# Computing the Mamba step sizes inside the keys-and-values chunk of a fused two-layer backbone, and reordering the input stage around it

## The chip, the cores and the metric

One core of one Trainium2 chip runs the whole program. The metric is device time of one execution in microseconds. TensorE (PE) does the matrix products, ScalarE (ACT) and VectorE (DVE) read PSUM and write SBUF, GpSimd (POOL) adds a few blocks, SyncE (SP) issues the loads.

## The reference, cut to what matters

Two layers run over 256 latent and 256 context tokens with 1024 features, all in fp32. Each layer starts with one input projection, whose columns go to three mixers:

```python
proj = h @ p['w_in']                    # columns: k, v, xb, dt, C, q, z, hyena
dt = softplus(dt_raw + dt_bias)         # dt_raw: 16 columns, two directions x 8 heads
a_dt = dt * a;  a_cs = cumsum(a_dt)     # decays of the Mamba scan
y = y * silu(z);  y = rmsnorm(y) * g    # gate at the end of the Mamba mixer
```

The three mixers' outputs are normalized, joined, projected and added to the stream; a SwiGLU follows. In layer 1 (the second) the context tokens are needed only for keys, values, the xb columns and dt.

## The kernel before, in words

Every weight is used as a pair: `w_hi` is the raw piece rounded to fp32r by ACT (`round_w`, L1481), and `w_lo` is the rest, which DVE makes (`split_w`, L1854). A product is three matmuls (hi x hi, hi x lo, lo x hi). Weights come in pieces of 512 KB into a ring of four slots (`RING = 4`). SP loads a piece once PE has counted `w_used` for the piece four places back; ACT rounds it, DVE splits it, PE waits for `w_lo_done`.

The input stage of each layer has 30 pieces, two for each of the 15 chunks in `W_IN`: three xb chunks and C (kind `xbc`), then z (two chunks), kv (one), q (two), hyena (six). Products land in two pairs of PSUM banks, (0, 1) and (2, 3). A chunk opens its pair with `pair_open`, which waits until the reader of the chunk before the last has counted `pair_free`. For `xbc` and `hy` chunks ACT starts the short convolution (L1548) and DVE finishes it (L2035, L2039) and frees the pair. A z chunk is read by ACT with Silu (L1557), kv by DVE copies (L2052, L2053).

The first two chunks are made together by `h_pair` (L834, L835, L841), as h becomes ready block by block. Behind it `step_sizes` (L952, L953) makes the 16 step-size columns for all tokens: a 128x32 weight (hi and lo side by side, made by POOL from a load of its own, `load_wdt`) against h_hi and h_lo, 16 matmuls of 512 columns. DVE copies the 32 rows (L2015), PE turns them to tokens with `dsel` (L999), and DVE and ACT make dt, its logarithm and dt·a (L2084 to L2092, L1575 to L1578).

The order of the small work is written out by hand: `at_piece(s)` and `in_piece(s)` on PE, and a loop over s = 2 to 31 on ACT and on DVE, where step s reads the chunk that ended with piece s-1, rounds or splits piece s+2, and then does what the constants assign to it: `S_DT` = 5 the step sizes, `S_CUMS` = 6 cumulative sums (L1004 to L1010, L2121 to L2131), `S_XS0`, `S_XS1`, `S_B` = 7, 8, 9 transposes (L1024), `S_G` = 11 the products of B and C (L1032), `S_HEAD` = 12 the first of eight decay matrices (one for each piece: L963, L965 on PE, L1612 on ACT, L2146, L2147 on DVE, L983 on PE), `S_STATE` = 13 the first of twelve state steps (L1073, L1080, L2154 to L2167), `S_GATE` = 25 the gate (L2240), `S_GATE + 1` the root mean square on ACT (L1462 to L1464), `S_FEAT` = 29 the transposes of the result (L862). In layer 0 five spectra of the Hyena filter are made at pieces 10 to 12 (`filter_spectrum`, L918 and L922, one bank, each copied by DVE at L2116 before the next may start); in DVE's step they come after the `S_DT` work. In layer 0 the projection runs over 512 tokens in every chunk, in layer 1 z, q and hyena run over 256.

Each engine takes its instructions strictly in order. ACT's tables have to be switched between Silu and the set with exponential and logarithm (`ACT_TABLE_LOAD`).

Of the kernel before, what the change touches and what calls it, by code (L numbers as in the profile page):

```python
# [17 lines left out]
P = 128  # L18
D = 1024
# [23 lines left out]
        + [("z", OFF_Z + CW * i, i) for i in range(2)] + [("kv", OFF_K, 0)]  # L43
# [7 lines left out]
STAGES = [("in", 30, 15), ("out", 12, 4), ("gu0", 24, 12), ("down0", 12, 4), ("gu1", 20, 10), ("down1", 12, 4)]  # L51
RING = 4

# [14 lines left out]
def piece_cols(i):  # L68


    for l in range(DEPTH):
        g = PLAN[l, "down1"][0]
        if g <= i < g + 12:
            return CW * (4, 3, 3)[(i - g) % 3]
    return 4 * CW
# [3 lines left out]
S_DT, S_CUMS, S_XS0, S_XS1, S_B, S_G, S_HEAD, S_STATE, S_GATE, S_FEAT = 5, 6, 7, 8, 9, 11, 12, 13, 25, 29  # L79
# [6 lines left out]
SPEC_BANKS = (1, 6, 7, 4, 5)  # L86
# [161 lines left out]
def backbone(nc, x, c, ctx_in, c_ctx, w_mod, b_mod, norm1_g, w_in, ssd_conv_w, ssd_conv_b, ssd_a_log,  # L248
# [3 lines left out]
    with ExitStack() as stack:  # L252
# [12 lines left out]
        w_raw, w_lo = at("w_raw", 48, [RING, 4 * CW]), at("w_lo", 48, [RING, 4 * CW], F32R)  # L265
        w_hi = at("w_hi", 64, [RING, 4 * CW], F32R)
        m_raw = at("m_raw", 80, [2, 4 * CW])
        m_big = [at("m_even", 80, [8 * CW]), at("m_odd", 144, [8 * CW])]


        xbc = at("xbc", 88, [8, T])
        ysum, xw = at("ysum", 88, [4, 512]), at("xw", 96, [2, 512])
        hyv, x0, x1t = at("hyv", 104, [4, T]), at("x0", 112, [4, T]), at("x1t", 120, [2, T])
        zs = at("zs", 124, [4, 512])
        qk, v_nat = at("qk", 132, [4, QKW]), at("v_nat", 142, [4, 2 * HD])
        spec = at("spec", 144, [5, 512])
        csT, csr = at("csT", 154, [T]), at("csr", 154, [T], F32R)
        gT, bnat = at("gT", 156, [2, 4, P]), at("bnat", 160, [4, GN])
        xsn = at("xsn", 164, [4, 512])
        em = at("em", 172, [4, T])  # L280
        st = at("st", 180, [2, 512])


        f_hi, f_lo = at("f_hi", 88, [12, T], F32R), at("f_lo", 112, [12, T], F32R)
        att_lo, hy_lo = at("att_lo", 156, [4, T], F32R), at("hy_lo", 164, [4, T], F32R)
        gate, hidden = at("gate", 136, [2, T]), at("hidden", 140, [2, T])
        sqr, rstd, lnt = at("sqr", 172, [2, T]), at("rstd", 176, [T]), at("lnt", 178, [T])
        hf = at("hf", 180, [2, T])

        c_sq = at("c_sq", 184, [4, P])  # L290
        maskb, identb = at("maskb", 186, [2, P], BF16), at("identb", 186.5, [P], BF16)
        c_fwd = at("c_fwd", 187, [5 * P + 3])
        c_inv = at("c_inv", 193, [2 * NFREQ, P])
        c_rope = at("c_rope", 197, [2, 2, HD])
        gcoss = [at(f"gcos{l}", kb, [2, 2, HD]) for l, kb in enumerate((156, 201.5))]
        gsins = [at(f"gsin{l}", kb, [2, 2, HD]) for l, kb in enumerate((157, 202.5))]
# [4 lines left out]
        wdts = [at(f"wdt{l}", kb, [8, 16]) for l, kb in enumerate((154, 176))]  # L301
        wdt_hl = at("wdt_hl", 201.5, [8, 32], F32R)
# [12 lines left out]
        dsel = at("dsel", 207.6875, [16])  # L315
        hsqs, hbuf = at("hsqs", 112, [2, QKW]), at("hbuf", 112, [2, QKW])
        ropt = at("ropt", 117, [QKW])
        qkT = at("qkT", 132, [4, 5, P])


        t_filt, t_sum, t_diff = at("t_filt", 104, [2, D]), at("t_sum", 112, [2, 512]), at("t_diff", 116, [2, 512])
        t_mod = at("t_mod", 148, [2, CW])
        t_hyb = at("t_hyb", 152, [512])
        t_half, t_hyb1 = at("t_half", 180, [D]), at("t_hyb1", 178, [512])
        t_sum1, t_diff1 = at("t_sum1", 164, [2, 512]), at("t_diff1", 168, [2, 512])

        t_folds = [at(f"t_fold{l}", kb, [4, 512]) for l, kb in enumerate((104, 156))]
        t_w3, t_decay = at("t_w3", 156, [D]), at("t_decay", 160, [2, 512])
        t_arg, t_k, t_h = ([at(f"{name}{l}", kb + off, shape) for l, kb in enumerate((144, 172))]
                           for name, off, shape in (("t_arg", 0, [L]), ("t_k", 1, [L]), ("t_h", 2, [2, L])))  # L330
        t_w1, t_w2, t_feats = at("t_w1", 168, [HD]), at("t_w2", 168.25, [HD]), at("t_feats", 168.5, [L])
        t_mask = at("t_mask", 169.5, [2, P])
        m_acc, m_pick = at("m_acc", 152, [2, MOD_COLS]), at("m_pick", 205, [2, 32])
        m_first = [at(f"m_first{m}", kb, [2, MOD_COLS]) for m, kb in enumerate((80, 112, 120, 128, 136, 88, 96, 104))]
# [4 lines left out]
        vn, yspecs = at("vn", 16, [4, 512]), [at("yspec0", 24, [NFREQ, 512]), at("yspec1", 172, [NFREQ, 512])]  # L339
# [2237 lines left out]
```

## Time and profile before

| | us |
|---|---|
| median of three runs | 1227.86 (1227.34 to 1228.2) |
| the profiled execution: its own time | 1227.09 |
| its span, first to last instruction | 1225.0 |
| PE busy | 1186.8 (97%) |
| DVE busy | 828.6 (68%) |
| ACT busy | 523.9 (43%) |
| POOL busy | 12.5 (1%) |

Times in rows count from the start of the span. In a timeline row the columns are start, duration of the merged group, engine, line, operation, output<-input, shape and count; square brackets hold the idle time of that engine before the row and what released it. A matmul's duration overlaps the next one, so the cost of a group is the distance of the starts. The input stage of layer 0 lies at about 29 to 262 us, that of layer 1 at 796 to 939 us.

### The profile page before, as it was taken

What the parts mean: (1) busy time and instruction counts of PE and PEld (TensorE: products, weight loads), DVE (VectorE), ACT (ScalarE), POOL (GpSimd) and SP (SyncE); (2) the same over time, 40 slices, a digit from 0 to 9 for tenths busy, and PEclk for the clock granted to TensorE, in tenths of its full rate; (3) what the DMA queues carried; (4) which work ended last, traced back from release to release, by engine and by line L of the source; (5) the groups of instructions that cost most, each with busy time, mean ns of one, the idle gap of its engine ahead of it and who ended that gap; (6) DMA issues with size and microseconds to landing.
All of it is one profiled execution on the core that took longest, in us unless ns stands there. A gap on an engine that the chain in (4) does not pass through costs nothing. (4 is left out here: it accounts for less than half of the span.)

```text
span 1225.0 us, 16695 instructions
## 1 busy us (share of the span) xinstructions
PE 1186.8 (97%) x6746; PEld 954.8 (78%) x6746; DVE 828.6 (68%) x1298; ACT 523.9 (43%) x907; POOL 12.5 (1%) x16
## 2 busy tenths in 40 slices
PE   5999999999999999999999999999989998999998
PEld 3667777777677788888887778678888688889888
DVE  5755457869766748677556665575699876776674
ACT  4453544552544532231122232366575555443454
POOL 0000000000000000000000000000000000000000
PEclk9999999999999999999999999999999999999999
DMA  9834243421012255556656454324334133665553
GB/s 337 265 121 137 87 138 123 154 69 52 19 35 70 69 172 187 184 179 206 196 187 198 145 190 155 95 69 123 102 108 134 53 86 100 194 189 184 183 180 125
DMA packets 132388, 171.36 MB, mean 140 GB/s; under 512 B 9268, under 2 KB 112342, under 8 KB 132312
## 3 DMA queue, kind: packets, MB, share of 16 engines
q1 hardware_dynamic: 131828, 170.12, 43.2%
q8 instruction: 53, 0.87, 0.3%
q10 hardware_dynamic: 484, 0.18, 0.1%
q14 instruction: 23, 0.19, 0.0%
HBM read 169.24 MB, written 1.05 MB: 139 GB/s over the span
## 5 line engine op out<-in xcount | busy, mean ns | idle before, releaser
L1854 DVE TENSOR_TENSOR w_lo<-w_raw,w_hi 128x1024 fp32r<-128x1024 f32 (+1 forms) x220 | 264.3, 1206 | 161.9 <-ACT w_hi L1481 159.9
L1481 ACT ACTIVATE w_hi<-w_raw 128x1024 fp32r<-128x1024 f32 (+1 forms) x220 | 228.8, 1043 | 328.2 <-DMA w_raw<-in_w_gu_dram 142.5
L730 PE MATMUL ps<-h_hi,w_hi 128*128 128x512 f32 (+1 forms) x576 | 218.7, 380 | 0.9 <-DVE w_lo L1854 0.6
L732 PE MATMUL ps<-h_hi,w_lo 128*128 128x512 f32 (+1 forms) x576 | 212.7, 369 | 0.0
L731 PE MATMUL ps<-h_lo,w_hi 128*128 128x512 f32 (+1 forms) x576 | 212.4, 369 | 0.0
L730 PE MATMUL ps<-f_hi,w_hi 128*128 128x512 f32 (+1 forms) x472 | 168.0, 356 | 2.7 <-DVE xT L2273 2.5
L732 PE MATMUL ps<-f_hi,w_lo 128*128 128x512 f32 (+1 forms) x472 | 162.8, 345 | 0.0
L730 PEld LDWEIGHTS ps<-h_hi,w_hi 128*128 128x128 f32 x576 | 108.5, 188 | 26.9 <-issue 8.8
L732 PEld LDWEIGHTS ps<-h_hi,w_lo 128*128 128x128 f32 x576 | 108.5, 188 | 18.8
L731 PEld LDWEIGHTS ps<-h_lo,w_hi 128*128 128x128 f32 x576 | 108.6, 189 | 17.4
L741 PE MATMUL ps<-h_hi,w_hi 128*128 128x512 f32 x320 | 113.2, 399 | 0.4 <-ACT gate L1786 0.4
L730 PEld LDWEIGHTS ps<-f_hi,w_hi 128*128 128x128 f32 x472 | 89.6, 190 | 19.3 <-issue 4.7
L732 PEld LDWEIGHTS ps<-f_hi,w_lo 128*128 128x128 f32 x472 | 89.5, 190 | 11.0
L731 PE MATMUL ps<-f_lo,w_hi 128*128 128x512 f32 (+1 forms) x240 | 90.1, 375 | 0.0
L742 PE MATMUL ps<-h_hi,w_lo 128*128 128x256 f32 x320 | 89.9, 281 | 0.0
L741 PEld LDWEIGHTS ps<-h_hi,w_hi 128*128 128x128 f32 x320 | 60.1, 188 | 15.5 <-DVE w_lo L1854 0.6
L742 PEld LDWEIGHTS ps<-h_hi,w_lo 128*128 128x128 f32 x320 | 60.5, 189 | 0.0
L731 PEld LDWEIGHTS ps<-f_lo,w_hi 128*128 128x128 f32 x240 | 45.2, 188 | 8.2 <-issue 0.5
L2491 DVE SCALAR_TENSOR_TENSOR m_acc<-m_odd,cact,m_acc 128x1024 f32<-128x1024 f32 x40 | 50.2, 1281 | 0.5
L1670 ACT ACTIVATE prob<-ps,sm 128x512 f32<-128x512 f32 (+1 forms) x48 | 29.1, 612 | 40.4 <-DVE sm L2315 37.9
L2454 DVE TENSOR_TENSOR hidden<-gate,ps 128x1024 f32<-128x1024 f32 (+1 forms) x12 | 14.1, 1176 | 41.5 <-PE ps L732 38.2
L1132 PE MATMUL ps<-w_hi,h_hi 128*128 128x512 f32 x96 | 40.4, 421 | 0.5 <-DVE xbc L2039 0.5
(349 smaller groups left out, 1904.6 us busy)
## 6 DMA issues: line engine op xcount, KB each, us to landing
w_raw<-in_w_gu_dram SPq DMA_DIRECT2D x88, 512.0 KB, 3.6
w_raw<-in_w_in_dram SPq DMA_DIRECT2D x60, 512.0 KB, 3.8
w_raw<-in_w_down_dram SPq DMA_DIRECT2D x32, 512.0 KB, 3.4
m_even<-in_w_mod_dram SPq DMA_DIRECT2D x14, 1024.0 KB, 6.0
m_odd<-in_w_mod_dram SPq DMA_DIRECT2D x14, 1024.0 KB, 5.9
m_raw<-in_w_mod_dram SPq DMA_DIRECT2D x24, 512.0 KB, 5.3
m_first<-in_w_mod_dram SPq DMA_DIRECT2D x16, 512.0 KB, 10.4
w_raw<-in_w_out_dram SPq DMA_DIRECT2D x16, 512.0 KB, 3.4
```

Source lines behind the costliest of these rows:

```text
L730: mm(o, w_hi[:, i % RING, w], hi[:, 0:n], start=first and k == 0, stop=False)
L731: mm(o, w_hi[:, i % RING, w], lo[:, 0:n], start=False, stop=False)
L732: last = mm(o, w_lo[:, i % RING, w], hi[:, 0:n], start=False, stop=final and k == nk - 1)
L741: mm(o, w_hi[:, i % RING, w], both(k), start=first and k == 0, stop=False)
L742: last = mm(o[:, 0:L], w_lo[:, i % RING, w], both(k)[:, 0:L], start=False, stop=final and k == nk - 1)
L1132: mm(o, h_hi[:, b, tok], w_hi[:, (i + half) % RING, w], start=(b == 0), stop=False)
L1481: A(w_hi[:, i % RING, w], w_raw[:, i % RING, w], ACT.Copy).then_inc(w_hi_done, 1)
L1670: p.sig(A(prob[:, i % 2, j, 0:keys], ps[:, 4 + j, 0:keys], ACT.Exp, bias=sm[:, 0, c:c + 1], accum_out=sm[:, 1, c:c + 1]), "probs_ready")
L1854: TT(w_lo[:, i % RING, w], w_raw[:, i % RING, w], w_hi[:, i % RING, w].bitcast(F32), ALU.subtract).then_inc(w_lo_done, 1)
L2454: TT(hidden[:, :, 0:n], gate[:, :, 0:n], ps[:, 2 * ((q + 1) % 2):2 * ((q + 1) % 2) + 2, 0:n], ALU.mult).then_inc(pair_free[(q + 1) % 2], 1)
L2491: ins = STT(out=acc, in0=src, scalar=by, in1=acc, op0=ALU.mult, op1=ALU.add)
```

## The change

Step sizes stop being a product of their own. The kv chunk becomes `KVW` = 272 columns wide (256 of keys and values, 16 of dt), all ring slots grow to `SLOT` = 1088 columns, and each kv piece is loaded by two DMAs (256 and 16 columns). One token tile with 272 columns fills a bank, so kv takes two pairs instead of one, and the input stage has 16 pairs. kv moves ahead of z (pieces 8 and 9; z at 10 to 13). `load_wdt`, POOL's two operations, `step_sizes`, the copy, `dsel` and the turning matmuls go; DVE adds the bias while it reads kv. `h_pair` ends chunk 0 ahead of chunk 1 in its last three blocks of the second half (it is also used in the SwiGLU stages), and ACT and DVE handle pieces 4 and 5 only after chunk 0's convolution. z is copied from PSUM without Silu and gets it in SBUF at step 22. The hand-written order shifts.

```diff
-        + [("z", OFF_Z + CW * i, i) for i in range(2)] + [("kv", OFF_K, 0)]
+        + [("kv", OFF_K, 0)] + [("z", OFF_Z + CW * i, i) for i in range(2)]
-S_DT, S_CUMS, S_XS0, S_XS1, S_B, S_G, S_HEAD, S_STATE, S_GATE, S_FEAT = 5, 6, 7, 8, 9, 11, 12, 13, 25, 29
+S_DT, S_CUMS, S_XS0, S_XS1, S_B, S_G, S_HEAD, S_STATE, S_ZS, S_GATE, S_FEAT = 10, 11, 7, 8, 9, 12, 13, 14, 22, 26, 29
...
+                    both = (4, 1)[half]
+                    for k in range(both):
...
+                    for k in range(both, 4):
+                        p.after("h_hi_ready")
+                        of_hi(k, 0)
+                        p.after("h_ready")
+                        of_lo(k, 0)
+                    for k in range(both, 4):
+                        of_hi(k, 1)
+                        of_lo(k, 1)
...
                     if s == S_CUMS:
                         p.after("adt_ready")
+                        p.after("xsn_ready", l + 1)
...
                     if s == S_G:
                         p.after("conv_ready")
-                        p.after("xsn_ready", l + 1)
+                        p.after("csr_ready")
+                        p.after("decays_ready")
...
-                step_sizes()
...
+                            if u == count:
+                                pair_open(q + 1)
...
+                            if u == count - 1:
+                                p.sig(last, "kv_psum")
...
-                    if s == 2:
-                        round_w(g0 + 4)
-                        round_w(g0 + 5)
...
-                            act.wait_ge(w_used, g0 + max(2 * ch + 2, 4))
+                            act.wait_ge(w_used, g0 + (3, 4)[ch] if ch < 2 else g0 + 2 * ch + 2)
...
+                        if s == 2:
+                            round_w(g0 + 4)
+                            round_w(g0 + 5)
...
-                                ins = A(zs[:, t, :], ps[:, 2 * ((q - 1 + t // 2) % 2) + t % 2, :], ACT.Silu)
+                                ins = A(zs[:, t, :], ps[:, 2 * ((q - 1 + t // 2) % 2) + t % 2, :], ACT.Copy)
...
+                    if s == S_ZS:
+                        for q in (pair_of(6) - 1, pair_of(6)):
+                            act.wait_ge(pair_free[(q0 + q) % 2], (q0 + q) // 2 + 1)
+                        p.sig(A(zs[:, 0:tiles, :], zs[:, 0:tiles, :], ACT.Silu), "zs_ready")
...
+                def read_kv(q, half):
...
+                    V.tensor_copy(v_nat[:, tt, :], src[:, :, P:CW])
+                    V.tensor_copy(qk[:, tt, 512:QKW], src[:, :, 0:P])
+                    TT(dtr[:, tt, :], src[:, :, CW:KVW], bc16[:, l, 0:1, :].to_broadcast([P, 2, 16]), ALU.add).then_inc(pair_free[q % 2], 1)
+
...
+                    if s == 2 * KV_CHUNK + 1:
+                        if l == 0:
+                            dve.wait_ge(late_full, 16 * LATE_LOADS)
+                        p.after("kv_psum")
+                        read_kv(q0 + KV_CHUNK, 0)
```

## Rows read from the trace of the kernel before

**Rows 1.** Stretches of layer 1: length, then busy time and instructions of each engine, clock, DMA.

```profile
871.66:889.34 17.68, 17.45 (x90) 13.29 (x90) 12.55 (x24) 9.60 (x23) 0.00 (x0) 1.00 0.47 136
889.34:938.75 49.41, 45.43 (x348) 43.48 (x349) 46.13 (x100) 33.51 (x78) 0.00 (x0) 1.00 0.44 128
```

**Rows 2.** Timeline of PE, layer 1: first step-size matmul, chunk 2, the turning.

```profile
817.17 0.39 PE L952 MATMUL ps<-h_hi,wdt_hl 128*32 128x512 f32 x1
817.40 0.39 PE L953 MATMUL ps<-h_lo,wdt_hl 128*32 128x512 f32 x1
...
821.19 0.47 PE L730 MATMUL ps<-h_hi,w_hi 128*128 128x512 f32 x1 [0.17 <-DVE xbc L2039]
...
826.80 1.06 PE L999 MATMUL ps<-dsel,csT 32*128 32x16 f32 x8
```

**Rows 3.** Timeline of ACT and DVE: convolution of chunk 0 in layer 1, two splits in layer 0.

```profile
817.37 1.45 ACT L1548 ACTIVATE xbc<-ps,vecT 128x512 f32<-128x512 f32 x2 [5.05 <-PE ps L841]
...
819.64 1.41 DVE L2039 SCALAR_TENSOR_TENSOR xbc<-ps,vecT,xbc 128x510 f32<-128x510 f32 x2
...
257.72 2.35 DVE L1854 TENSOR_TENSOR w_lo<-w_raw,w_hi 128x1024 fp32r<-128x1024 f32 x2
```

**Rows 4.** Timeline, layer 1: end of kv, reload of the slot of its first piece, rounding.

```profile
870.42 0.28 PE L1153 MATMUL ps<-w_lo,h_hi 128*128 128x256 f32 x1
870.54 0.28 PE L1154 MATMUL ps<-w_hi,h_lo 128*128 128x256 f32 x1
...
872.96 1.06 ACT L1481 ACTIVATE w_hi<-w_raw 128x1024 fp32r<-128x1024 f32 x1 [8.13 <-DMA w_raw<-in_w_in_dram]
```

**Rows 5.** Timeline: step-size chain of layer 1; end of kv and next rounding in layer 0.

```profile
828.04 0.48 DVE L2084 MEMSET csr<- 128x512 f32 x1
...
829.81 0.22 DVE L2091 TENSOR_TENSOR adt<-dt,bc 128x64 f32<-128x64 f32 x1
...
143.13 0.28 PE L1154 MATMUL ps<-w_hi,h_lo 128*128 128x256 f32 x1
...
145.95 1.06 ACT L1481 ACTIVATE w_hi<-w_raw 128x1024 fp32r<-128x1024 f32 x1 [7.54 <-DMA w_raw<-in_w_in_dram]
```

**Rows 6.** Timeline of layer 0, piece 10: first two spectra and the copy between.

```profile
107.81 1.08 PE L918 MATMUL ps<-t_fold,c_fwd 128*64 128x512 f32 x4
...
108.94 0.69 DVE L2116 COPY spec<-ps 128x512 f32<-128x512 f32 x1 [0.85 <-PE ps L918]
...
111.68 1.02 PE L922 MATMUL ps<-t_fold,c_fwd 128*128 128x512 f32 x2
```

**Rows 7.** Timeline of layer 1: waits of PE, reading z, the table switch, the first head.

```profile
846.53 0.47 PE L1132 MATMUL ps<-w_hi,h_hi 128*128 128x512 f32 x1 [0.53 <-DVE xbc L2039]
...
855.92 1.09 ACT L1557 ACTIVATE zs<-ps 128x512 f32<-128x512 f32 x2 [1.16 <-PE ps L1134]
...
857.15 0.35 PE L1152 MATMUL ps<-w_hi,h_hi 128*128 128x256 f32 x1 [0.63 <-ACT zs L1557]
...
857.97 1.28 ACT L1604 ACT_TABLE_LOAD   x1
...
859.26 1.14 ACT L1612 ACTIVATE em<-ps,bia 128x128 f32<-128x128 f32 x4
...
860.28 2.45 ACT L1619 ACTIVATE ysum<-xsn,bc 128x128 f32<-128x128 f32 x8
```

**Rows 8.** Timeline: gate, norm and transposes at the end, layer 1 then layer 0.

```profile
927.12 1.29 DVE L2240 TENSOR_TENSOR ysum<-ysum,zs 128x512 f32<-128x512 f32 x2
...
930.52 1.34 ACT L1653 ACTIVATE ysum<-ysum,st 128x512 f32<-128x512 f32 x2
...
935.00 1.03 PE L862 MATMUL ps<-c_sq,ysum 128*128 128x128 f32 x8
...
251.35 1.67 DVE L2246 TENSOR_SCALAR ysum<-ysum,st 128x512 f32<-128x512 f32 x4
...
259.88 1.48 PE L862 MATMUL ps<-c_sq,ysum 128*128 128x128 f32 x12
```

More of the change, by code:

```diff
@@ L121, in half_after, with pair_of @@
     return h if 0 <= h < PARTS - 3 else None
+def pair_of(ch):
+    return ch + (ch > KV_CHUNK)
 def loads_into(i):
-    return i // RING + 1 + sum(i >= PLAN[l, "out"][0] + PARTS + (i - PLAN[l, "out"][0]) % RING for l in range(DEPTH))
+    wide = [PLAN[l, "in"][0] + 2 * KV_CHUNK + half for l in range(DEPTH) for half in range(2)]
+    return i // RING + 1 + sum(i >= g and i % RING == g % RING for g in wide) + sum(i >= PLAN[l, "out"][0] + PARTS + (i - PLAN[l, "out"][0]) % RING for l in range(DEPTH))
 def gate_up(part, f, r):
@@ L286, in backbone @@
[L286 to L292, printed above, removed]
+        w_raw, w_lo = at("w_raw", 48, [RING, SLOT]), at("w_lo", 48, [RING, SLOT], F32R)
+        w_hi = at("w_hi", 65, [RING, SLOT], F32R)
@@ new lines, in of_hi @@
+                    def of_hi(k, c):
+                        s = (g + 2 * half + c) % RING
+                        for j in range(2):
+                            o = ps[:, 2 * ((q + c) % 2) + j, 0:n]
+                            w = slice(k * CW + j * P, k * CW + (j + 1) * P)
+                            mm(o, w_hi[:, s, w], h_hi[:, 4 * half + k, 0:n], start=(half == 0 and k == 0), stop=False)
+                            mm(o, w_lo[:, s, w], h_hi[:, 4 * half + k, 0:n], start=False, stop=False)
@@ new lines, in of_lo @@
+                    def of_lo(k, c):
+                        s = (g + 2 * half + c) % RING
+                        lo = h_lo[:, 4 * half + k, 0:n] if n == T else h_hi[:, 4 * half + k, L:T]
+                        for j in range(2):
+                            w = slice(k * CW + j * P, k * CW + (j + 1) * P)
+                            last = mm(ps[:, 2 * ((q + c) % 2) + j, 0:n], w_hi[:, s, w], lo, start=False, stop=(half == 1 and k == 3))
+                        if k == 3:
+                            last.then_inc(w_used, 1)
@@ L945, in _ @@
                     p.after("spec_ready")
-                def step_sizes():
-                    pe.wait_ge(wdt_split, l + 1)
-                    for k in range(KD):
-                        mm(ps[0:32, 6, :], wdt_hl[:, k, :], h_hi[:, k, :], start=(k == 0), stop=False)
-                        last = mm(ps[0:32, 6, :], wdt_hl[:, k, :], h_lo[:, k, :], start=False, stop=(k == KD - 1))
-                    p.sig(last, "dt_psum")
                 def cum_rows(h):
```

200 lines of the change are left out of this document (80 added, 120 removed).

## Prediction

> **What bounds the kernel now.** I read the page first: PE is busy for 97% of the span, by the table above, so a matmul that goes is a gain unless a new wait takes its place. Next the stretches of layer 1's input stage. From the first q piece to the end of its last piece there are two: in the first DVE has 12.55 busy of 17.68 us, in the second 46.13 of 49.41, and PE is idle there for 49.41 - 45.43 = 4.0 us [rows 1]. So PE sets the early part, and DVE's queue nearly sets the late part. Then I read the timelines engine by engine around what the change moves.
>
> **What goes.** In each layer 16 step-size matmuls stand between `h_pair` and chunk 2. They start at 817.17, 0.23 us apart, and chunk 2 starts at 821.19 [rows 2]: 4.0 us, of which 16 x 0.23 = 3.7 is their own and the rest a wait for chunk 0's convolution, which they covered. The turning matmuls cost 1.0 us more [rows 2]. Together 5.0 us a layer.
>
> **What the cover was worth.** Chunk 2 needs chunk 0's pair free and piece 4 split. Before, ACT began chunk 0 at 817.37, 0.20 after `h_pair`'s end E, and DVE finished at 819.64 + 1.41 = 821.05, so 3.68 after ACT's start [rows 3]. Now chunk 0 ends 18 matmuls x 0.227 = 4.1 us before E; ACT starts at E - 3.9, DVE ends at E - 0.2. But the split of piece 4 now stands behind that convolution: 1.2 us (half of the two in 2.35) [rows 3], to E + 1.0, and PE starts at about E + 1.1. Cost 1.1 a layer; ends 0.3 and 1.5, the lower if the pair alone decides.
>
> **The wider chunk.** 96 matmuls go from 256 to 272 columns. A step of 512 columns is 0.23 us [rows 2], one of 256 is 0.12 [rows 4], 0.41 ns a column: 96 x 16 x 0.41 ns = 0.6 us a layer. Nothing shows 272; ends 0 (if the weight load sets the step) and 1.5.
>
> **What is queued behind kv.** This decides. PE counts `w_used` for kv's first piece only after the seventh of its eight parts, so the slot that piece 12 needs is free late. Before, piece 16 had that place: ACT rounded it at 872.96, while kv's last matmul was done at K = 870.54 + 0.12 = 870.66, so rounding began at K + 2.3 [rows 4]. In layer 0 it was 145.95 against 143.25, K + 2.7 [rows 5]. With the last part 0.1 longer I take K + 2.2 and K + 2.6. The new `S_DT` = 10 is behind exactly that piece on both engines: on ACT behind `round_w(12)`, on DVE behind `split_w(12)`.
>
> Layer 1: rounding to K + 3.3, splitting to K + 4.5. Then the chain that took 829.81 + 0.22 - 828.04 = 2.0 us from the memset to dt·a [rows 5]; without the bias addition 1.8. dt·a is ready at K + 6.25, and PE's cumulative sums can start at K + 6.4. PE arrives there after one z piece, 12 matmuls of 512 columns with its start-up, at K + 2.9. Stall 3.5 us. The next link (sums, then `csr_ready` before `S_G`) is again one such piece; I give it 0.2.
>
> Layer 0: pieces are twice as long, so the sums are in time, but the second spectrum is not. It needs the first one's copy, and that copy stands behind the `S_DT` work in DVE's queue. Rounding to K + 3.7, splitting to K + 4.9, table load 1.28 [rows 7] on ACT and the exponential of the decay rates in parallel to K + 5.2, two small DVE operations, memset from K + 5.55, dt·a by 7.2, its last small operation, then the copy of 0.69 [rows 6] to K + 8.1; PE goes on at K + 8.3. PE arrives 111.68 - 107.81 = 3.9 us after piece 10's start [rows 6]. Stall 4.4 us. Ends for both stalls: 2 lower in each if the reload were faster, 1 higher in each.
>
> **Waits that leave.** PE waited 0.53 us for the convolution of C and 0.63 for ACT's reading of z [rows 7]. Both readers get a longer cover: -1.2 in layer 1.
>
> **Reading z later.** z is now read at step 14, behind head 0's exponentials (1.14) and the eight `ysum` copies (2.45) [rows 7], and the q chunk after it needs its pair. Before, 12 us of kv covered those copies. With H the start of step 13 on PE: ACT rounds piece 15 until H + 1.5, exponentials to H + 2.65, copies to H + 5.05, z's two copies (1.09) [rows 7] to H + 6.1. PE is ready at H + 4.2 (one z piece, decay matrix 1, head 0). Stall about 2.0 in layer 1; ends 0 and 3.3 (one table load more, should the repeated preload not be dropped). In layer 0 the piece is 2.8 us longer and PE has enough to do: 0.
>
> **The shift by one piece.** In layer 1 the heads and states move one piece later, so 2.1 us of DVE work (one head, one state step) moves from in front of step 18 into the stretch where DVE is busy 46.13 of 49.41 [rows 1]. Against it stand the 5.1 us that DVE idled in the stretch before, partly behind the late piece 16. By my walk over steps 14 to 18 PE reaches step 18 no later than before, with that work outstanding: the extra stalls here and the recovered ones cancel with the 1.3 us that the terms so far leave layer 1 behind. I take 0 beyond the 1.3; ends -2 and +2.
>
> **The end of the stage.** The gate moves from 25 to 26, `S_FEAT` stays 29. In layer 1 the gate began at 927.12, the norm was done at 930.52 + 1.34 = 931.86 (4.7 us), and PE needed it at 935.00: 3.1 us to spare [rows 8]. The gate now comes after the convolution and split of step 26 (3.6 us later), and the z Silu at 22 has put the wrong table in, so a load of 1.28 us [rows 7] is on this path. 4.9 - 3.1 = 1.8 of stall at most, if nothing else moved; as DVE's other work moves forward by what the gate left, I take 1.2; ends 0 and 2.6. In layer 0 the norm (1.67) now follows the convolution of step 28 and a split: 257.72 + 1.2 + 1.67 = 260.6 against 259.88 [rows 3, 8]: 0.8, ends 0 and 1. The Silu itself (2.1 us in layer 0 for 2048 columns, by twice the 1.06 that ACT takes for 1024) goes at no cost: ACT is busy for 33.51 of the 49.41 us of its stretch [rows 1], and only the table switch, counted above, meets the path.
>
> The Trainium skill (ScalarE: Activation LUTs, section What ACT_TABLE_LOAD costs) says that a switch costs the load of 1283 ns and a drain of about 1380 more. In this trace the load is 1.28 us, and the exponential starts at 859.26, 0.01 after the load's end [rows 7]: the load agrees, the drain does not show. By the page the sum would be up to 2.8 us higher, since the switch ahead of the norm is on the path once in each layer.
>
> **Nothing on the path.** DMA bytes are the same; the 16-column loads add packets, for which I allow 0.1 at kv's start in each layer; ends 0 and 1.5. POOL's work was covered. In the SwiGLU stages the new order of `h_pair` frees the gate earlier, but ACT reaches it only after two roundings, so 0. Other bank numbers and addresses cost nothing by any row.
>
> **Sum.** Layer 0: -5.0 + 1.1 + 0.6 + 0.1 + 4.4 + 0.8 = +2.0. Layer 1: -5.0 + 1.1 + 0.6 + 0.1 + 3.5 + 0.2 - 1.2 + 2.0 + 0 + 1.2 = +2.5. The profiled execution took 1227.1 us (span 1225.0 and 2.1 around it), so 1227.1 + 4.5 = 1231.6; it lay 0.8 under the median of the three runs. I forecast 1231.5. 0.2% is 2.5 us, about what a measurement of this kernel can tell from no change.
>
> **Rivals.** *The late terms are hidden (25%).* The two stalls behind kv come as worked out, but z's late reading is absorbed, since the DVE queue sets layer 1's end anyway, and the gate is in time. Without 2.0, 1.2 and 0.8: +0.5, about 1227.7. For it speaks that DVE idles 5.1 us ahead of its full stretch [rows 1]; against it that the gate's slack of 3.1 is smaller than its delay.
>
> *The step-size chain is short (20%, faster).* It decides at kv's end, by when piece 12 can be rounded. If that piece had landed by K, dt·a would be ready at about K + 0.35 + 1.0 (reading kv) + 1.2 + 1.8 = K + 4.4, a stall of 1.6 in layer 1; in layer 0 2.5 us less, 1.9. That is 4.4 less in all, and with hidden late terms as above 8.4 less: 1223 to 1227, middle 1224. The point from which it turns the sign: both stalls together under about 4 us with the late terms hidden. For it: reloads elsewhere are rounded as late only because ACT was busy. Against it: ACT waited 8.13 and 7.54 us for just this piece in both layers [rows 4, 5], so it was the DMA.
>
> *A table switch costs more than its load (5%, slower still).* If a switch on the path also drains, the two norms start 1.4 us later each: +2.8, 1234.4. The 0.01 us gap speaks against it. The page named above is what speaks for it.
>
> **How the numbers follow.** The forecast keeps 50%, the rivals 25, 20 and 5. Slower by over 0.2%: 50 + 5 = 55%; within it 25%; faster 20%. The forecast's own ends (all stalls lower or higher together) are about 1228.5 to 1235. The range takes in the hidden case and most of the short chain: 1223.5 to 1235.
>
> **What would show it.** Right: no L952 or L999; chunk 2 waiting about 1 us on w_lo; in layer 1 a PE idle of 3 to 4 us ahead of the cumulative sums, released by dt·a on DVE; in layer 0 about 4 us ahead of the second spectrum, released by DVE's copy of the first spectrum (L2116); ACT waiting for DMA at the rounding after kv; PE idle about 2 us ahead of layer 1's first q piece, released by ACT's copy of z; a short idle ahead of the transposes at the end. Wrong: if PE passes kv's end in both layers with under 2 us of idle in the next two pieces, the short chain is true and the time is below 1226; if the end of layer 1's stage keeps to its 4 us of idle, the late terms are hidden.

## The result, and the profile after

The changed kernel takes 1250.14 us (median of four runs, 1248.93 to 1253.32) against 1228.03 for the kernel before, measured beside it. The ratio is 1.0188, 95% interval 1.0174 to 1.0201: slower by 22 us. The forecast was 1231.5 with a range up to 1235.0, so the sign was right and the size was not. The profiled execution has a span of 1246.8 us, 21.8 more than the one before.

The page's busy line for the kernel after says where to look. PE is busy for as long as before, to 0.5 us, so its idle time has grown by 22.3 us (the span less the busy time: 60.5 against 38.2). That does not mean that it has as much to do: matmuls have gone, and a part of the rest ran at the lower clock, as shown below. And ACT has 22.5 us more work, of which the diff tells nothing.

```profile
PE 1186.3 (95%) x6698; PEld 956.0 (77%) x6698; DVE 827.5 (66%) x1297; ACT 546.4 (44%) x925; POOL 10.9 (1%) x12
```

Next, rows of PE in the two input stages of the kernel after, ahead of which it waited and in the kernel before did not, or far less. The brackets hold the idle time and its releaser.

```profile
76.22 1.12 PE L913 MATMUL ps<-t_w,t_h 64*128 64x512 f32 x2 [1.55 <-DVE t_filt L2102]
...
113.27 1.11 PE L926 MATMUL ps<-t_fold,c_fwd 128*128 128x512 f32 x2 [4.08 <-DVE spec L2116]
...
266.38 0.85 PE L866 MATMUL ps<-c_sq,ysum 128*128 128x128 f32 x6 [2.63 <-issue]
...
826.81 0.47 PE L731 MATMUL ps<-h_hi,w_hi 128*128 128x512 f32 x1 [0.87 <-DVE w_lo L1850]
...
864.71 0.41 PE L995 MATMUL ps<-adt,c_sq 128*128 128x32 f32 x2 [3.54 <-DVE adt L2091]
...
878.79 0.38 PE L958 MATMUL ps<-csr,pick 40*128 40x256 f32 x1 [1.11 <-ACT em L1604]
...
882.68 0.77 PE L1120 MATMUL ps<-w_hi,h_hi 128*128 128x512 f32 x1 [1.80 <-ACT zs L1549]
...
953.71 0.51 PE L866 MATMUL ps<-c_sq,ysum 128*128 128x128 f32 x2 [3.97 <-issue]
```

Four of these are waits of the forecast, at their places and near its sizes: chunk 2 on `w_lo` (0.87), the second spectrum of layer 0 (4.08), the cumulative sums of layer 1 (3.54), the first q piece (1.80). The two ahead of the norm's transposes (L866; 2.63 and 3.97) are at the forecast's place and far above its size. Those at 76.22 and 878.79 were not foreseen.

The queue behind kv is as it was worked out. These are ACT and DVE in layer 1 of the kernel after, K being 858.2:

```profile
860.55 1.06 ACT L1473 ACTIVATE w_hi<-w_raw 128x1024 fp32r<-128x1024 f32 x1 [7.04 <-DMA w_raw<-in_w_in_dram]
861.63 1.28 ACT L1562 ACT_TABLE_LOAD   x1
...
861.64 1.23 DVE L1850 TENSOR_TENSOR w_lo<-w_raw,w_hi 128x1024 fp32r<-128x1024 f32 x1 [2.25 <-ACT w_hi L1473]
...
864.43 0.23 DVE L2091 TENSOR_TENSOR adt<-dt,bc 128x64 f32<-128x64 f32 x1
```

ACT waits 7.04 us for piece 12's load, rounds at K + 2.3, DVE splits, and dt·a starts at K + 6.2. In the kernel before the rows to hold against these are [rows 4, 5].

Two things come on top. The first is the clock. Here are windows of the kernel after around three of the waits; behind POOL's column stands the clock that PE was granted (1.00 is 2.4 GHz, 0.50 is 1.2 GHz).

```profile
core 0: us, PE busy (x) PEld busy (x) DVE busy (x) ACT busy (x) POOL busy (x), PEclk, DMA share, GB/s
...
109.00:113.20 4.20, 0.18 (x1) 0.00 (x0) 3.02 (x10) 2.32 (x6) 0.00 (x0) 1.00 0.40 156
113.20:115.00 1.80, 1.74 (x10) 0.70 (x14) 0.58 (x1) 0.56 (x1) 0.00 (x0) 0.78 0.04 9
115.00:117.00 2.00, 2.00 (x14) 0.93 (x7) 1.24 (x2) 0.00 (x0) 0.00 (x0) 0.50 0.00 0
117.00:119.00 2.00, 2.00 (x8) 1.57 (x8) 0.00 (x0) 0.00 (x0) 0.00 (x0) 0.84 0.00 0
...
864.60:866.00 1.40, 1.29 (x14) 1.12 (x18) 0.16 (x2) 1.20 (x2) 0.00 (x0) 0.70 0.00 0
866.00:868.00 2.00, 2.00 (x19) 1.34 (x12) 1.85 (x5) 1.06 (x3) 0.00 (x0) 0.50 0.00 0
868.00:870.00 2.00, 2.00 (x8) 1.59 (x8) 1.07 (x3) 1.93 (x6) 0.00 (x0) 0.86 0.00 0
...
953.60:956.00 2.40, 2.29 (x12) 2.32 (x13) 1.81 (x4) 2.40 (x5) 0.00 (x0) 0.56 0.00 0
956.00:958.00 2.00, 2.00 (x14) 2.00 (x14) 1.09 (x3) 1.87 (x5) 0.00 (x0) 0.67 0.00 0
```

PE was idle for about 4 us, and the work behind it ran partly at the lower level. PE's busy time times the missing clock gives 1.7 us behind each of the three, and 1.5 behind the wait at 882.68 (0.50 and 0.59 in its two windows): 6.6 us in all. The kernel before loses 1.7 us in the same way, at one place of layer 1's output stage (last section), where the changed kernel loses nothing, so the difference is 4.9. The forecast priced the waits at their idle time alone. The mean granted clock was 0.989 to 0.993 in the four runs of the changed kernel, and 0.994 to 0.999 in the 56 runs of the kernel before beside the experiments.

The second is ACT's tables. The page counts 18 more ACT instructions; the kernel before had 15 `ACT_TABLE_LOAD`, the one after has 31. The timeline of ACT at the norm of layer 1, in the kernel after:

```profile
949.14 1.28 ACT L1455 ACT_TABLE_LOAD   x1
950.44 0.29 ACT L1455 ACTIVATE st<-st,eps 128x2 f32<-128x2 f32 x1
950.75 1.28 ACT L1456 ACT_TABLE_LOAD   x1
952.05 0.20 ACT L1456 ACTIVATE st<-st 128x2 f32<-128x2 f32 x1
952.28 1.33 ACT L1649 ACTIVATE ysum<-ysum,st 128x512 f32<-128x512 f32 x2
```

The logarithm comes with one load and the exponential behind it with another. The same happens at the two norms of the output stage (L1679, L1680) and at the stream's norm (L1428, L1429): four roots a layer, two loads each, 16 x 1.28 = 20.5 us of ACT. It ends in each layer at the SwiGLU's own switch.

How far the profiled executions lie behind the one before, in us, at the end of the same piece (e1, e3 and e7 are experiments of the next section):

| end of | after | e1 | e3 | e7 |
|---|---|---|---|---|
| layer 0, piece 0 | 0.8 | 0.8 | 0.7 | 1.7 |
| layer 0, piece 7 | -3.6 | -3.6 | -3.7 | -4.0 |
| layer 0, piece 14 | 2.0 | 1.9 | -1.4 | -3.2 |
| layer 0, piece 28 | 3.7 | 3.6 | 0.4 | -2.3 |
| layer 0, piece 29 (behind the transposes) | 6.5 | 4.4 | 1.1 | -2.3 |
| layer 1, piece 0 | 8.6 | 4.3 | 1.3 | -2.0 |
| layer 1, piece 7 | 3.1 | -1.3 | -4.3 | -7.6 |
| layer 1, piece 14 | 12.4 | 7.9 | -2.6 | -5.7 |
| layer 1, piece 28 | 14.6 | 10.1 | -0.4 | -5.0 |
| layer 1, piece 29 | 20.3 | 11.7 | 1.2 | -5.0 |
| the span | 21.8 | 14.4 | 4.7 | -6.0 |

At the first row no product that the change touches has run yet; executions differ there by themselves (0.3 us in e11, 0.8 in e9). The 1.7 of e7 there is a stretch at half clock in its profiled execution, at 23.7 us.

### The profile page after: what moved, and what is told of

Read it like the earlier page. It is cut to its first block and busy times, and to the rows that moved or that the text cites. A ratio compares the mean times of both kernels' runs of the same rounds, so it can differ in the third digit from the quotient of the medians.

```text
span 1246.8 us, 16616 instructions
## 1 busy us (share of the span) xinstructions
PE 1186.3 (95%) x6698; PEld 956.0 (77%) x6698; DVE 827.5 (66%) x1297; ACT 546.4 (44%) x925; POOL 10.9 (1%) x12
## 5 line engine op out<-in xcount | busy, mean ns | idle before, releaser
L1850 DVE TENSOR_TENSOR w_lo<-w_raw,w_hi 128x1024 fp32r<-128x1024 f32 (+2 forms) x220 | 264.2, 1206 | 157.8 <-ACT w_hi L1473 155.6
L1473 ACT ACTIVATE w_hi<-w_raw 128x1024 fp32r<-128x1024 f32 (+2 forms) x220 | 227.9, 1043 | 313.6 <-DMA w_raw<-in_w_gu_dram 144.1
L731 PE MATMUL ps<-h_hi,w_hi 128*128 128x512 f32 (+1 forms) x576 | 219.3, 381 | 1.9 <-DVE w_lo L1850 1.7
L743 PEld LDWEIGHTS ps<-h_hi,w_lo 128*128 128x128 f32 x320 | 60.5, 189 | 0.0
L831 PE MATMUL ps<-h_hi,w_hi 128*128 128x512 f32 (+1 forms) x112 | 39.7, 363 | 3.8 <-ACT h_hi L1437 3.2
```

What stands on the lines that cost most here:

```text
L731: mm(o, w_hi[:, i % RING, w], hi[:, 0:n], start=first and k == 0, stop=False)
L743: last = mm(o[:, 0:L], w_lo[:, i % RING, w], both(k)[:, 0:L], start=False, stop=final and k == nk - 1)
L831: mm(o, w_hi[:, s, w], h_hi[:, 4 * half + k, 0:n], start=(half == 0 and k == 0), stop=False)
L1473: A(w_hi[:, i % RING, w], w_raw[:, i % RING, w], ACT.Copy).then_inc(w_hi_done, 1)
L1850: TT(w_lo[:, i % RING, w], w_raw[:, i % RING, w], w_hi[:, i % RING, w].bitcast(F32), ALU.subtract).then_inc(w_lo_done, 1)
```

## The experiments

Each set ran beside the kernel before on one chip, and times of different sets are compared by their ratios to it. The kernel before took 1227.17 us (e1 to e4), 1227.73 (e5 to e8) and 1227.44 (e9 to e11).

### e1 and e2: the tables, out of the changed kernel and into the one before

e1 is the changed kernel with one line more:

```diff
                     if s == S_ZS:
...
                         p.sig(A(zs[:, 0:tiles, :], zs[:, 0:tiles, :], ACT.Silu), "zs_ready")
+                        act.preload_act_table_set("natural_log_exp_and_others")
```

> The changed kernel plus one explicit preload of the table set with both logarithm and exponential directly behind the SBUF Silu of z. Theory A (the unforecast time is the table loads): in the changed kernel every logarithm and every exponential of the four reciprocal roots per layer loads a table of its own, 16 loads more than before, 8 at the norm of y and of the attention, Hyena and stream norms in layer 0 and 8 in layer 1. With the preload there are 31 - 16 + 2 = 17 loads, the idle of PE ahead of the transposes of the norm falls from 2.8 (layer 0) and 4.1 us (layer 1) by two loads, 2.6, each, and the growth of 2.1 and 1.5 us after the input stages goes: 5.1 + 3.6 = 8.7, so 1241 to 1243 us. Rival B (the loads lie in ACT's idle time and the late gate is bound by DVE's queue): under 3 us are saved, 1247 or more.

Measured: 1243.60 us, ratio 1.0145 (1.0130 to 1.0159), 0.0043 or 5.3 us under the changed kernel, where 7 to 9 were expected; the span is 7.4 us shorter. PE's idle time falls by 8.6 us (60.5 to 51.9, by the two pages), close to the expected 8.7. But e1 loses 3.0 us to the clock behind a wait of 2.73 us in layer 1's output stage (1026.38), where the changed kernel waits 1.19 and loses nothing. The norm of layer 1 in e1, on ACT and on PE:

```profile
944.65 0.29 ACT L1455 ACTIVATE st<-st,eps 128x2 f32<-128x2 f32 x1
944.98 0.20 ACT L1456 ACTIVATE st<-st 128x2 f32<-128x2 f32 x1
...
946.64 0.52 PE L866 MATMUL ps<-c_sq,ysum 128*128 128x128 f32 x3 [1.40 <-issue]
```

No load is left at the roots (17 in all), and PE's wait ahead of the transposes falls from 3.97 to 1.40, by the two loads. That 1.40 is the late gate alone. The forecast's 1.2 was meant to hold the gate and one load of 1.28, so the gate's part was too small as well.

e2 is the opposite: the kernel before, and nothing but a forced switch.

```diff
                     if s == S_HEAD + HEADS + 1:
                         p.after("y_head_done", 2)
+                    if s == 22:
+                        act.preload_act_table(ACT.Silu)
```

> The kernel before plus nothing but a preload of the Silu table at step 22 of each input stage: no arithmetic changes. Theory A: the logarithms and exponentials of the roots behind it load singly, 15 + 2 + 16 = 33 loads or close to it, and the kernel before is slower by 6 to 12 us (about 1234 to 1240), with PE idle ahead of the norm's transposes. Rival B: within 1.5 us of 1228.

Measured: 1234.88 us, ratio 1.0068 (1.0056 to 1.0080), so one line makes the kernel before 8 us slower. Its timeline of ACT shows the pair of loads at a norm that had none [rows 8]:

```profile
932.49 1.28 ACT L1463 ACT_TABLE_LOAD   x1
933.78 0.30 ACT L1463 ACTIVATE st<-st,eps 128x2 f32<-128x2 f32 x1
934.10 1.28 ACT L1464 ACT_TABLE_LOAD   x1
935.39 0.20 ACT L1464 ACTIVATE st<-st 128x2 f32<-128x2 f32 x1
```

It has 33 loads in all, as expected. Theory A holds on both sides; a miss is only where the cost falls. In e2 PE waits under 1 us around the transposes, because the gate there is early; the loss comes behind the input stages.

### e3: the step-size work ahead of piece 12

e3 is e1 with the work of `S_DT` moved, unchanged, in front of the rounding on ACT and of the splitting on DVE:

```diff
+                    if s == S_DT:
+                        act.preload_act_table_set("natural_log_exp_and_others")
...
                     if 4 <= s < 30:
                         round_w(g0 + s + 2)
...
-                    if s == S_DT:
-                        act.preload_act_table_set("natural_log_exp_and_others")
...
```

> As the first of this set, with the step-size work of step 10 ahead of the rounding and the splitting of piece 12 on ACT and DVE. Theory A (the idle of PE ahead of the cumulative sums is the queue behind the late slot of piece 12): dt*a no longer waits for the DMA; the 3.7 us of layer 1 fall to about 0.5, the 1.3 us ahead of the next decay matrix to under 0.5, and the 4.2 us ahead of the second spectrum of layer 0, whose copy still stands behind the split, fall by the 2.5 us of the step-size work: 6 us in all, so about 1236. Rival B (the chain of reading the keys, values and step sizes sets it, not the slot): under 2 us are gained.

Measured: 1230.42 us, ratio 1.0031 (1.0019 to 1.0043), 13.2 us under e1 on the same chip, twice what was expected. PE's waits in e3:

```profile
111.45 1.10 PE L926 MATMUL ps<-t_fold,c_fwd 128*128 128x512 f32 x2 [2.36 <-DVE spec L2117]
...
859.57 0.68 PE L1021 MATMUL ps<-xbc 128*128 128x128 f32 x4 [1.28 <-DVE csr L2129]
...
869.07 0.47 PE L1120 MATMUL ps<-w_hi,h_hi 128*128 128x512 f32 x1 [1.19 <-ACT zs L1549]
```

The wait ahead of the cumulative sums is gone, so it was the queue, and the chain alone is short. In layer 1 three waits of e1 (3.56, 0.74 and 1.80) have become the last two above, 3.6 us less; in layer 0 3.97 has become 2.36. That is 5.2 us of idle, and the spans differ by 9.7: the rest is the clock. The same stretch of time in e1, then in e3, which is some 10 us further in its work:

```profile
865.00:890.00 25.00, 22.12 (x102) 16.75 (x101) 11.93 (x20) 13.71 (x33) 0.00 (x0) 0.93 0.33 89
```

```profile
865.00:890.00 25.00, 23.57 (x130) 18.57 (x129) 14.86 (x29) 16.87 (x43) 0.00 (x0) 1.00 0.42 125
```

Three slow stretches of e1, behind its waits at 113.18, 860.36 and 877.96, are gone, 1.7 us each, which fits. The medians differ by 3.5 us more than the two spans. The mean granted clock of the runs explains most of it: in e1 it is 0.992 in the profiled run and 0.9905 in the median of the runs, in e3 0.996 and 0.997. In the 56 runs of the kernel before, a clock lower by 0.001 goes with a time longer by 1.0 us, so by this estimate 2.5 of the 3.5 us are the clock. The rest stays open.

### e4: the copies that start ysum, one step earlier

```diff
-                    if s == S_HEAD:
+                    if s == S_G:
                         p.own("xsn_ready")
                         for h in range(HEADS):
...
                     if s == S_G:
                         p.after("g_psum")
```

> As the third, with the eight copies that start ysum from the xb columns moved from step 13 to step 12, ahead of the wait for the products of B and C. Theory A (PE's 2.0 us ahead of the first q piece in layer 1 is z's reading queued behind those copies): that idle goes, 2.0 us faster than the third, about 1234. Rival B (DVE's full queue in the second half of layer 1's stage takes it back): the idle goes and reappears at steps 18 to 24, less than 0.5 us is gained.

Measured: 1230.00 us, ratio 1.0028 (1.0015 to 1.0040), 0.4 under e3. The wait of 1.19 us ahead of the first q piece is gone, and the profiled span is 2.0 us shorter, but the medians show almost none of it. Of the 2.0, 1.0 is won in layer 1's input stage and still there at its end; 1.3 are the clock in the output stage, which the edit does not touch (e3 loses 3.0 us there, e4 1.7). Theory A is right on the place and cause of the wait; by the medians whether its time stays won is open, as the difference lies inside the spread of the runs.

### e5: the wait filled with empty matmuls

e5 is e1 with this in front of PE's wait:

```diff
                     if s == S_CUMS:
-                        p.after("adt_ready")
                         p.after("xsn_ready", l + 1)
+                        for k in range(14 if l == 1 else 0):
+                            mm(ps[:, 6, :], h_hi[:, k % 8, 0:P], h_hi[:, k % 8, 0:T], start=True, stop=True)
+                        p.after("adt_ready")
```

> As e1, with 14 matmuls of 512 columns that nothing reads put in front of PE's wait for dt*a in layer 1, about 3.2 us of empty work in the place of 3.7 us of idle. Nothing else changes, dt*a comes at the same time. Theory C (an idle of some 4 us costs more than itself, because the clock granted behind it is the lower one): the stretch of about 3.5 us behind the wait, which ran at half the clock in the changed kernel and in e1, runs at 1.00, and the cumulative sums to the next z piece take 1.5 to 2 us less; the whole gains that, about 1242 against e1's 1243.6. Rival D (the slow stretch comes from what the matmuls wait for, or from the small matmuls there): the same 3.5 us stay slow, and the time stays as in e1.

Measured: 1239.20 us, ratio 1.0098 (1.0079 to 1.0116), 0.0047 or 5.8 us under e1. PE in e5, then its window behind the wait and the window of e1 at the same place:

```profile
858.25 3.33 PE L994 MATMUL ps<-h_hi 128*128 128x512 f32 x14
861.86 0.41 PE L997 MATMUL ps<-adt,c_sq 128*128 128x32 f32 x2 [0.27 <-DVE adt L2094]
```

```profile
862.00:864.00 2.00, 2.00 (x25) 1.61 (x26) 0.82 (x1) 1.77 (x4) 0.00 (x0) 1.00 0.00 1
```

```profile
862.00:864.00 2.00, 2.00 (x5) 1.53 (x5) 1.94 (x6) 1.77 (x7) 0.00 (x0) 0.50 0.00 0
```

dt·a comes no sooner, PE does 3.3 us of work for nothing, and the kernel is faster: theory C holds, rival D falls. From the end of piece 10 to that of piece 11, e5 takes 1.7 us less than e1, as expected. By piece 14 it is 3.9 less. The wait of 0.74 is gone, and so is the second slow stretch of e1, behind its wait of 1.80 ahead of the first q piece, though e5 has that wait too, with the same 1.80 us (877.28). So that wait alone does not lower the clock.

The spans differ by only 3.2 us, as e5's profiled execution has a slow stretch of its own, where the edit changes nothing. It lies behind the wait of 1.55 us for the filter's taps, which e1 has too: from 77 to 81 us PE is busy throughout in both, and its clock is 0.58 in e5 and 1.00 in e1. By this stretch alone e5 loses 1.7 us more.

### e6: first readings ahead of the splits, layer 0

On DVE, in e4, the first of each pair of tap products and of each pair of spectrum copies goes ahead of the split:

```diff
+                    if l == 0 and s in (S_TAPS, S_TAPS + 1):
+                        read_taps(s - S_TAPS, 0)
+                    if l == 0 and s in (S_SPEC, S_SPEC + 1, S_SPEC + 2):
+                        copy_spectrum(2 * (s - S_SPEC))
                     if 4 <= s < (30, S_FEAT - 1)[l] and state_at(s) is None:
                         split_w(g0 + s + 2)
```

> As e4, with DVE's first reading of each pair of filter taps and of each pair of spectra in layer 0 ahead of the split of its step. By the theory that PE's waits there (1.7 us ahead of the second taps, 2.5 us ahead of the second spectrum in e4) are DVE's queue, the first falls by 1.2 and the second to under 0.5: 3.2 us faster than e4, about 1227. By the rival (the splits come later and PE waits for w_lo instead) under 0.7 us are gained.

Measured: 1226.22 us, ratio 0.9991 (0.9980 to 1.0001), 0.0037 or 4.5 us under e4. Both waits are gone. At piece 14 layer 0 leads e4 by 4.1 us, of which 0.4 stood before the first piece, so 3.7 against 3.2 expected, and it stays so. The wait that no one had foreseen (76.22) was DVE's queue: in the kernel before PE came to the second pair of tap products at 79.8, in the changed kernel at 74.7, and there DVE's reading of the first stood behind a split.

### e7: states from 13, gate at 25

```diff
-S_DT, S_CUMS, S_XS0, S_XS1, S_B, S_G, S_HEAD, S_STATE, S_ZS, S_GATE, S_FEAT = 10, 11, 7, 8, 9, 12, 13, 14, 22, 26, 29
+S_DT, S_CUMS, S_XS0, S_XS1, S_B, S_G, S_HEAD, S_STATE, S_ZS, S_GATE, S_FEAT = 10, 11, 7, 8, 9, 12, 13, 13, 22, 25, 29
...
-                    if s == S_HEAD:
+                    if s == S_G:
                         p.after("gT_ready")
                         weigh(0, 0)
```

> As e6, with the states from piece 13 and the gate at 25 again, as before the change, so that a state step, the gate, the norm and the scaling come one piece earlier. If the late gate holds PE ahead of the transposes (1.6 us in layer 1 and 0.7 us in layer 0 in e4), these go: 2.3 us faster than e6, about 1225. If DVE's full queue in the second half of layer 1's stage sets the end whatever the order, the idle moves to steps 18 to 24 and less than 0.5 us is gained.

Measured: 1221.84 us, ratio 0.9951 (0.9935 to 0.9967), the fastest kernel of this study, 6 us under the one before. Three of PE's waits in layer 1:

```profile
856.55 0.68 PE L1021 MATMUL ps<-xbc 128*128 128x128 f32 x4 [1.57 <-DVE csr L2138]
...
865.99 0.47 PE L1120 MATMUL ps<-w_hi,h_hi 128*128 128x512 f32 x1 [0.24 <-ACT zs L1549]
...
927.04 0.39 PE L731 MATMUL ps<-h_hi,w_hi 128*128 128x256 f32 x1 [0.34 <-DVE w_lo L1851]
```

No wait stands ahead of the transposes any more; layer 1's stage is 2.0 us shorter than e6's and layer 0's 0.6, 2.6 together against 2.3 expected. By the ratios e7 gains 4.9. Another 1.3 is won at the start of layer 1's output stage, where e6 waits 1.07 us for DVE's `f_lo` (936.17) and e7 under 0.5. The clock takes no part in the two spans: each of the two executions loses 1.7 us to it, e6 in the output stage and e7 at the start. The remaining 1.0 is not explained.

### e8 and e9: what the step-size matmuls covered

e8 is the kernel before with 2 of its 16 step-size matmuls:

```diff
-                    for k in range(KD):
-                        mm(ps[0:32, 6, :], wdt_hl[:, k, :], h_hi[:, k, :], start=(k == 0), stop=False)
-                        last = mm(ps[0:32, 6, :], wdt_hl[:, k, :], h_lo[:, k, :], start=False, stop=(k == KD - 1))
+                    mm(ps[0:32, 6, :], wdt_hl[:, 0, :], h_hi[:, 0, :], start=True, stop=False)
+                    last = mm(ps[0:32, 6, :], wdt_hl[:, 0, :], h_lo[:, 0, :], start=False, stop=True)
```

> The kernel before with 2 of the 16 step-size matmuls of each layer; it leaves out the product over all but the first of eight blocks of features, so the step sizes are not the reference's. By the forecast's reading (these matmuls covered the convolution of chunk 0, which frees chunk 2's pair 3.7 to 3.9 us after the pair ends), 14 x 0.23 = 3.2 us a layer leave PE's work and come back as a wait ahead of chunk 2: within 1 us of before, about 1227 to 1228, so the order of the two first chunks is what makes the gain. By the rival (the pair is free sooner and the cover was worth little) up to 6.4 us are gained, about 1221.

Measured: 1230.96 us, ratio 1.0025 (1.0012 to 1.0039). With 28 matmuls less the kernel is 3 us slower, where it was expected within 1 us of the one before. The wait of layer 0 in e8, and its clock:

```profile
62.21 0.76 PE L730 MATMUL ps<-h_hi,w_hi 128*128 128x512 f32 x1 [3.39 <-DVE xbc L2038]
```

```profile
62.00:64.00 2.00, 1.79 (x4) 1.49 (x5) 0.79 (x3) 1.90 (x3) 0.00 (x0) 0.50 0.05 17
64.00:66.00 2.00, 2.00 (x6) 1.55 (x5) 1.97 (x4) 2.00 (x3) 0.00 (x0) 0.50 0.00 0
```

The 3.2 us of matmuls come back as idle, as expected, and the clock makes it a loss: 3.1 us behind this wait and 1.7 behind the same one in layer 1 (825.84). The profiled execution is one of e8's slower ones (1234.43).

e9 is e8 with the change's `h_pair`, and on ACT and DVE pieces 4 and 5 behind the convolution of chunk 0 (the diff of the change has these lines).

> As e8 (2 of 16 step-size matmuls, so the step sizes are not the reference's), with the change's order of the first two chunks and the convolution of chunk 0 ahead of rounding and splitting pieces 4 and 5. By the forecast's reading the idle of 3.6 us ahead of chunk 2 in both layers falls to about 1 us less what two matmuls cover, so to 0.5, and the slow stretch behind it goes with it: 2 x (3.1 + 1.7) = 9.6 us faster than e8, about 1221 to 1223. By the rival (the order of the stores into the pairs or the later splits cost as much) it stays within 2 us of e8.

Measured: 1223.02 us, ratio 0.9962 (0.9948 to 0.9977), 0.0063 or 7.7 us under e8, where 9.6 were expected. The wait falls to 0.36 us on `w_lo`. e9's lead over the kernel before is made in the two input stages alone, 3.0 us in each by piece 7; from the end of layer 0's input stage to the start of layer 1's, where the new order of `h_pair` is at work in the SwiGLU, the two kernels agree within 0.1 us. So the gain of the change is real: the matmuls may go once the order of the two chunks is changed, and only then.

### e10 and e11: two variations of e7

e10 has the work of `S_CUMS` ahead of the rounding and splitting of piece 13, moved as the work of `S_DT` in e3.

> As e7, with the work on the cumulative sums of step 11 ahead of the rounding and splitting of piece 13. If the 1.7 us that PE waits ahead of the products of B and C in layer 1 are that queue, they go: about 1220, 1.5 us under e7. If the chain of small copies sets them, or the later split holds PE at piece 13, within 0.7 us of e7.

Measured: 1223.69 us, ratio 0.9969 (0.9957 to 0.9981); e7's is 0.9951 (0.9935 to 0.9967). The wait of 1.57 us is gone, one of about 0.7 stands ahead of a decay matrix instead, and the time does not fall. The rival comes nearer, but the intervals overlap, so it is not settled whether e10 is slower. In the stretch of the edit, layer 1 from piece 7 to 14, e10 is 0.8 us shorter than e7; its profiled execution loses 3.2 us more to the clock elsewhere, ahead of the first piece and in layer 1's output stage. The mean granted clock of e10's runs is 0.994, that of e7's 0.996. Why was not tried.

e11 is e7 without the line of e1.

> As e7, without the explicit preload behind the Silu of z. Theory A (each logarithm and exponential of the eight roots loads its own table): 31 loads instead of 17, and the time goes up by what the preload gave in e1, 6.5 us, to about 1228; PE is idle over 2 us again ahead of the norm's transposes in both layers. Rival: in a kernel without the other waits the loads find room, and under 3 us are lost.

Measured: 1227.19 us, ratio 1.0003 (0.9993 to 1.0012), 0.0052 or 6.4 us above e7. The size is theory A's. Its place for it is not: ahead of the transposes PE waits under 1 us. With an early gate the loads at the norm of y find room, and those of the output stage cost: behind layer 0's input stage, up to layer 1's, e11 falls back 1.9 us by the traces.

## Why the prediction was wrong

**What goes, and its cover: right.** In both layers chunk 2 waits just under 1 us on `w_lo` (0.82 and 0.87), against 1.1 forecast. e8 and e9 show that cover and gain are as reasoned.

**The wider chunk: right.** In layer 1 48 matmuls of 272 columns take 6.1 us where 48 of 256 took 5.8, so 0.6 for the two pieces, as forecast.

**The queue behind kv: right in place, cause and idle time.** Forecast 3.5 and 4.4 us, idle 3.54 and 4.08. e3 shows that the queue behind piece 12 makes them. The rival of a short step-size chain falls: it needed that piece early, and the load was as late as in [rows 4].

**Reading z later: right in place, its size partly luck.** 2.0 was forecast and 1.80 is the idle ahead of the q piece. But the forecast had head 0's exponentials end 2.65 us after H, the start of step 13 on PE. H is 874.21 here, and they end at 879.25, H + 5.0:

```profile
875.74 1.06 ACT L1473 ACTIVATE w_hi<-w_raw 128x1024 fp32r<-128x1024 f32 x1 [3.58 <-DMA w_raw<-in_w_in_dram]
876.82 1.28 ACT L1596 ACT_TABLE_LOAD   x1
...
878.11 1.14 ACT L1604 ACTIVATE em<-ps,bia 128x128 f32<-128x128 f32 x4
```

ACT rounded piece 15 about 1.1 us later than reckoned, as it waited for the load. And the second preload of the set, at `S_HEAD`, loaded its table again, though that set was in since 861.63; the forecast had taken it as dropped, with this case only in its end of 3.3. This delay is the wait of 1.11 us at 878.79: decay matrix 1 goes into the banks that head 0's exponentials read. Since PE was held there, it came late to the q piece too, and the wait for z kept its size. The two together are 2.9 us against 2.0. The rival of hidden late terms falls: neither of the late waits was absorbed.

**The step that failed first: "a load of 1.28 us (...) is on this path".** The forecast took the switch behind the Silu for one load, once, and read [rows 7] for its price. It did not ask which set the next logarithm would get. In the kernel before every logarithm and exponential stood behind an explicit preload of the set that holds both, with no Silu between. The Silu at step 22 took that set out, and with no preload behind it the logarithm and the exponential each came with a table of their own, at four roots a layer. The end of the stage was to cost 0.8 and 1.2 us and costs 2.63 and 3.97 of idle. Without the loads it costs 0.58 and 1.40 (e1). So layer 0's 0.8 was right without a load, and the late gate of layer 1, which by the forecast's own figures would have cost under 0.5 without its one load (3.6 of delay, 3.1 to spare), was too small by about 1. And 2.1 us of layer 0's loss and 1.5 of layer 1's come behind the input stage, where the forecast has nothing. e1 took back 5.3 us by the ratios and 7.4 by the spans; e2 and e11 give 8 and 6.4. The Trainium skill (ScalarE: Activation LUTs, section Table sets: the hidden batching unit) counts one load for a logarithm with an exponential behind it, since one set has both. In these traces that holds only where this set was loaded explicitly; behind the Silu of z there are two loads (949.14 and 950.75).

The drain, on which the 5% rival stood, does not show here either: where the function behind a load waits for nothing else, it starts 0.01 to 0.02 us behind the load's end (949.14 + 1.28 = 950.42, and 950.44). That rival's sum of 2.8 us was too small, and for the wrong reason.

**The second step that failed: that a stall costs its idle time.** The sum had "Stall 3.5 us", "Stall 4.4 us" and no word on the clock. Behind the long waits PE ran at 0.50 for some microseconds, 1.5 to 1.7 us more each, 6.6 in all in the profiled execution and 4.9 more than in that of the kernel before. e5 shows it by itself, and e3, which took out 5.2 us of idle, shortened the span by 9.7. The prices given in "Ends for both stalls" were too narrow for the same reason.

**Smaller misses.** The second taps of layer 0, not considered, waited 1.55, where they had waited for nothing. The link behind the cumulative sums, given 0.2, waited for nothing that shows (870.47). Between pieces 14 and 28 of layer 1 the changed kernel falls back by 2.2 us, but 1.5 of this is PE's own work, which the change moves there from ahead of piece 14: one head and one state step, with 10 matmuls of L958 in that stretch instead of 8 and 20 of the states instead of 16. PE's idle time there grows by 0.7, which is what the shift, taken as 0, cost at most.

The spans differ by 21.8 us, and the forecast's 4.5 leave 17.3 to explain. PE's time splits into idle, loss to the clock, and work at full clock. Its idle time grew by 22.3, its loss to the clock by 4.9, and its work (the busy time less the loss) fell by 5.3. The forecast's terms, split in the same way, are 12.5 more idle, nothing for the clock and 8.0 less work. So the idle was too small by 9.8, the clock by 4.9, and the saving of work too large by 2.7, of which 2.2 lie ahead of the end of the first piece, where no product has changed yet. Of the idle, the table loads are 8.6 (e1), the taps 1.55, the two waits at the first head 0.9 more than forecast, and the late shift 0.7; these come to 11.8, and smaller terms the other way take 2 of it back, 1.4 of them at that same place.

## What to carry to other kernels

Whoever moves a function that switches ACT's table must follow the tables on to the next explicit load and look whether each function behind it comes with a load of its own; one preload line gives it back. A preload of a set that is already in costs its load too. A stall on PE can cost, beyond its idle time, a stretch of half clock behind it, 1.7 us here behind each of the changed kernel's three waits of 3.5 to 4.1 us, and sometimes as much behind waits of 1.6 to 2.7. So it pays to put the small chain that PE waits for ahead of work that itself waits for a DMA. And matmuls that only cover a wait are worth removing only together with what removes the wait.

## What the runs showed of the hardware

Empty matmuls can make a kernel faster: e5 does 14 more than e1 and takes 5.8 us less by the ratios.

An explicit preload of a table set that is in already loads it again: in the changed kernel 861.63 and 876.82, with nothing of another set between.

The granted clock behind the same wait differs between executions. In layer 1's output stage PE waits for the squares, in three of the kernels about 2.6 us. In the kernel before it is 2.62 us (to 1013.23), and the clock then 0.57:

```profile
1005.00:1013.00 8.00, 5.60 (x47) 5.40 (x45) 5.25 (x8) 1.65 (x3) 0.00 (x0) 1.00 0.61 169
1013.00:1017.00 4.00, 3.77 (x15) 3.40 (x16) 2.01 (x3) 1.92 (x5) 0.00 (x0) 0.57 0.15 54
```

The missing 0.43 of 4 us are 1.7 us. In e6 the idle is 2.65 us and the clock 0.83 from 1005 to 1015, the same 1.7 us; in e7 it is 2.56 us, and the clock is full:

```profile
1005.00:1015.00 10.00, 7.44 (x56) 7.03 (x55) 5.74 (x9) 4.09 (x7) 0.00 (x0) 1.00 0.40 128
1015.00:1025.00 10.00, 9.86 (x66) 8.64 (x66) 6.53 (x14) 6.57 (x13) 0.00 (x0) 1.00 0.19 63
```

So one profiled execution compared with another can carry that much with nothing changed. The wait of 2.36 us in e3 at 111.45 left the clock at 1.00, while in e5 the wait of 1.55 us at 76.30 was followed by 0.58. The Trainium skill (TensorE: Matmul & The Clock Gate, section Part 1: The HAM clock gate) says that an idle array falls to half the clock. The traces agree where the clock falls, to 0.50 behind the long waits. Why the same 2.6 us lower it in one execution and not in the next was not tried here.
